# The smaller expert's second product moved ahead of the larger expert's last first products, with its load, in a two-block transformer kernel

## The reference

```
logits = t @ router                        # t: 256 x 1024, 8 experts
top_vals, top_idx = top_k(logits, 2)
gates = softmax(top_vals) placed at top_idx
for e in range(8):
    h_e = silu(t @ w1[e]) * (t @ w3[e])    # 1024 -> 3584
    out = out + gates[:, e] * (h_e @ w2[e])  # 3584 -> 1024
```

## Time and profile before

| what | value |
|---|---|
| median of three timed runs | 2823.32 us |
| profiled execution, its own time | 2816.06 us |
| span of that execution (first to last instruction) | 2814.2 us |
| PE busy (products) | 2723.3 us, 97% |
| DVE busy | 1684.4 us, 60% |
| ACT busy | 462.1 us, 16% |
| mean DMA rate over the span | 220 GB/s |
| chain that ended last, by engine | PE 86%, DVE 7%, DMA 4% |

### The profile page before, as it was taken

How to read it: one execution, slowest core, us unless ns; L and a number is a source line. 1 busy time by engine, 2 the same in 40 slices (tenths; PEclk the granted TensorE clock), 3 DMA queues, 4 the chain that set the end, 5 groups by cost and what they waited for, 6 DMA issues and landing times.

```text
span 2814.2 us, 48541 instructions
## 1 busy us (share of the span) xinstructions
PE 2723.3 (97%) x20880; PEld 2086.3 (74%) x20880; DVE 1684.4 (60%) x2934; ACT 462.1 (16%) x914; POOL 91.0 (3%) x130
## 2 busy tenths in 40 slices
PE   7999999999999999999998999988999999999997
PEld 6689878776678978777776887557777777777775
DVE  2554155776365416587554674237778878878876
ACT  2230212101212111200133111211111111111111
POOL 0011300000001120000000000000000000000000
PEclk9999999999999999999999999989999999999999
DMA  6242342543333135344333343329999999999995
GB/s 240 97 150 75 127 159 104 203 179 151 113 118 117 72 128 187 141 174 160 123 146 133 150 180 114 130 96 390 418 385 384 416 389 383 416 395 377 413 415 233
DMA packets 56940, 617.88 MB, mean 220 GB/s; under 512 B 6544, under 2 KB 6800, under 8 KB 8720
## 3 DMA queue, kind: packets, MB, share of 16 engines
q1 hardware_dynamic: 54576, 603.27, 54.5%
q0 software_dynamic: 2144, 11.45, 1.0%
HBM read 613.64 MB, written 1.05 MB: 218 GB/s over the span
## 4 chain that ended last, share of the span: by engine, by line
PE 86%; DVE 7%; DMA 4%; ACT 1%; issue 1%; SPq 0%; DVEq 0%; ACTq 0%
PE ps L1552 11%; PE ps L750 11%; PE ps L1232 10%; PE ps L1101 8%; PE ps L1244 8%; PE ps L1562 7%; PE ps L1576 5%; PE ps L1081 4%; PE ps L773 3%; PE ps L1598 3%; PE ps L731 2%; PE ps L1113 2%; DMA fbT<-in_od_exp_w 2%; PE ps L816 1%; PE ps L1210 1%; PE ps L1252 1%
## 5 line engine op out<-in xcount | busy, mean ns | idle before, releaser
L1101 PE MATMUL ps<-hT,slabA 128*128 128x256 f32 x1024 | 232.0, 380 | 1.1 <-ACT work L1837 1.1
L1101 PEld LDWEIGHTS ps<-hT,slabA 128*128 128x128 f32 x1024 | 192.2, 190 | 28.3 <-ACT work L1837 1.9
L1562 PE MATMUL ps<-fbT,work 128*64 128x256 f32 x1792 | 205.7, 382 | 2.8 <-DMA fbT<-in_od_exp_w 2.8
L1562 PEld LDWEIGHTS ps<-fbT,work 128*64 128x64 f32 x1792 | 124.1, 137 | 70.3 <-issue 11.0
L1552 PE MATMUL ps<-prm,hT 128*64 128x128 f32 x2688 | 167.4, 273 | 3.6 <-DVE resets L2965 2.9
L750 PE MATMUL ps<-hT,slabA 128*128 128x256 f32 x736 | 165.7, 385 | 1.0 <-DMA slabA<-in_od_w_in 0.5
L1552 PEld LDWEIGHTS ps<-prm,hT 128*64 128x64 f32 x2688 | 150.7, 136 | 13.6 <-issue 4.0
L750 PEld LDWEIGHTS ps<-hT,slabA 128*128 128x128 f32 x736 | 140.6, 193 | 21.6 <-issue 1.4
L1232 PEld LDWEIGHTS ps<-work 128*128 128x128 f32 x1152 | 139.5, 192 | 21.5 <-issue 21.0
L1232 PE MATMUL ps<-work 128*128 128x128 f32 x1152 | 143.9, 275 | 0.1
L750 PE MATMUL ps<-slabA,hT 128*128 128x512 f32 (+2 forms) x416 | 141.5, 496 | 2.2 <-ACT work L2024 1.8
(11 more groups left out here) (448 smaller groups left out, 4564.7 us busy)
## 6 DMA issues: line engine op xcount, KB each, us to landing
slabA<-in_od_exp_w SPq DMA_DIRECT2D x56, 2048.0 KB, 11.7
fbT<-in_od_exp_w SPq DMA_DIRECT2D x56, 2048.0 KB, 9.8
slabB<-in_od_exp_w SPq DMA_DIRECT2D x56, 1024.0 KB, 11.2
fbT<-in_od_exp_w SPq DMA_DIRECT2D x56, 1024.0 KB, 11.9
slabA<-in_w_in SPq DMA_DIRECT2D x24, 2048.0 KB, 8.2
slabA<-in_mlp_w SPq DMA_DIRECT2D x16, 2048.0 KB, 9.6
slabB<-in_mlp_w SPq DMA_DIRECT2D x32, 1024.0 KB, 4.8
slabA<-in_ev_ffn_w SPq DMA_DIRECT2D x11, 2048.0 KB, 7.9
```

Source lines behind the costliest of these rows:

```text
L1101: last = mm(ps[:, b, 0:T], side["gates"][:, k, c % 4 * P:(c % 4 + 1) * P], hT[:, k, :], start=(k == 0), stop=(k == KD - 1))
L1562: last = mm(ps[SMALL * j:SMALL * (j + 1), 1, 0:2 * P].rearrange("p (w n) -> p w n", w=2), xs[:, k, :], v[:, k, :, j * P:(j + 1) * P], star ...
```

## The change

The diff has three parts. On PE `down_b(g - 1)` moves from the end of a step to the place behind `up_b(g)`; its wait for `hidden_b` stands in it in every step, and the one in `extra` goes. In SP's queue `down_slab(g, 1)`, the load of B's second weights, moves from the last place of a step to the one behind the load of B's first weights. And in the first step `up_b(0)` no longer comes first: it runs inside `up_a(0, 0)`, behind the two products without sums and ahead of the wait for `sums_ready`.

```
@@ SyncE's queue
             for g in range(PAIRS * UPS):
                 up_slab(g + 1, 1)
+                down_slab(g, 1)
                 up_slab(g + 2, 0)
                 down_slab(g + 1, 0)
-                down_slab(g, 1)
@@ up_a
                     if c == 2 and part == 0:
+                        if g == 0:
+                            up_b(g)
                         pe.wait_ge(sem("sums_ready"), due("pe", "sums_ready"))
@@ down_b
-                if (g + 1) % UPS not in extras(g + 1):
-                    pe.wait_ge(sem("hidden_b"), due("pe", "hidden_b"))
+                pe.wait_ge(sem("hidden_b"), due("pe", "hidden_b"))
@@ extra
-                if i in extras(g):
-                    pe.wait_ge(sem("hidden_b"), due("pe", "hidden_b"))
@@ the steps on PE
                     if g == 0:
                         pe.wait_ge(sem("slots_a"), due("pe", "slots_a"))
-                        up_b(g)
                     up_a(g, 0)
                     if g:
                         turn(g - 1)
...
                     if g:
                         up_b(g)
+                        down_b(g - 1)
                     extra(g)
                     up_a(g, 1)
                     if g:
                         down_a(g - 1)
-                        down_b(g - 1)
```

## The result

Four runs of the changed kernel gave 2850.57 to 2854.46 us, median 2852.36; before, in four runs, 2823.33. The ratio is 1.0099 with a 95% interval of 1.0081 to 1.0116, so the change costs 29 us (23 to 33). The forecast was 2844, with a range of 2833 to 2856. Two runs of experiment 1, at 3270.75 and 4072.37 us with a mean granted clock of 0.82 and 0.65, are in none of the comparisons. The two profiled executions lie further apart, 2851.62 against 2816.06 us; of that distance of 35.6 us, 2.7 are there before the first expert is loaded (its first load is issued at 1892.67 us before and at 1895.36 after), in code that the change leaves alone.

What follows compares the result with a forecast made beforehand. PE was taken to set the step, with the loop through DVE and the transfers close behind; 22.1 + 3.9 + 0.9 + 1.0 - 3.7 - 2.8 = +21.4 us on the median 2823.3 gave 2844.7, stated as 2844, range 2833 to 2856.

Steps and rivals of the forecast that it cites:

- (d): Join on DVE: A's slab, issued D (sums' end) + 10.68, leaves 0.8 us spare; three pick steps add +1.0 us.
- (e): PE's nine short waits of B's second products for weights, and one for sums, go: -3.7 us (bounds -0.9, -4.2).
- (f): Tail: B's last second weights load earlier, DVE sets the order: -2.8 us, or -1.3 if the clock falls.
- (a): Steps 2 to 55: loop through ACT and DVE overruns its spare time by 0.41 us a step, +22.1 us.
- (b): Three scatter steps, where PE waits for DVE's y: each grows by the whole 1.72 us; +3.9 us beyond (a).
- (c): Start of B's second products: wait for hidden_b 0.3 us late only behind sums_of_slots, in 3 steps, +0.9 us.
- (g): First step: c = 0, 1 can start earlier, but sums still set c = 2; 0 us (bounds -0.3, +0.5).
- The third rival: A's slab, behind 1 MB more in the queue, sets the step: 16.2 us each, 2889 us; chance 0.05.
- the first (transfers pace the steps, 2813 us): Transfers set the step in the timed runs, and B's earlier load removes waits: 2813 us; chance 0.05.
- The second (the move does not reach the join): DVE comes late to the join for other reasons, so (a) is 0: 2821 us; chance 0.05.
- the fourth, the clock: A pause in each step drops PE to the half rate: 2908 us and more; chance 0.01.

Runs made afterwards that it cites:

- experiment 1: Changed kernel, c = 2 waiting only for the first two sums, sums of slots first in the first step: median 2827.8 us, ratio to before 1.001.
- experiment 6: Changed kernel with the old first step, B's first products first again: 2854.68 us, ratio to before 1.0104.
- experiment 5: Kernel before, B's second products moved from the step's end into the next step, behind c = 1: 2822.86 us, ratio 0.9999.
- Experiment 2: Changed kernel, loading only the first half of B's second weights in each step: 2844.47 us, ratio to before 1.0077.
- experiment 7: Kernel before, B's very last second weights loaded into the buffer of B's first weights: 2820.76 us, ratio 0.9984.
- the third kernel: Changed kernel with the load of B's second weights back in its old last place in SP's queue: 3060.51 us, ratio 1.0844.

## Why the prediction was right

The sign, the place and the plain step were right; one term was far off in size, (d), and two a little, (e) and (f). Time between the loads of c = 2 in step 1 and in step 55 was 851.0 us before and is 884.8 after, in the profiles. The sum by its own parts:

| part | forecast | in the profiles |
|---|---|---|
| (a) loop, steps 2 to 55 | +22.1 | +21.7 (53 steps of 0.40, one of 0.46) |
| (b) scatter steps | +3.9 | +3.9 (22.43 for 20.72) |
| (c) wait for hidden_b | +0.9 | +0.7 (3 of 0.24) |
| (d) late joins | +1.0 | +9.7 (11 steps) |
| (e) waits that go | -3.7 | -2.2 (what is left) |
| c = 2 of step 1 to c = 2 of step 55 | +24.2 | +33.8 |
| (f) tail | -2.8 | -1.0 |
| (g) first step | 0 | 0 (experiment 6) |

**(a)** holds by the timeline, by experiment 1, which took the loop away and with it the 0.40, and by experiment 5, which left the loop its cover. **(b)** The scatter's first products now wait longer for DVE's y:

```profile
2155.05 3.27 PE L1636 MATMUL ps<-work 64*128 64x512 f32 x14 [1.68 <-DVE work L3007]
```

1.68 us where it was 0.36: 1.32 more. **(c)** In the steps behind `sums_of_slots` the loads of B's second products stand right behind the copy:

```profile
2341.55 0.29 DVE L2979 COPY work<-ps 128x128 f32<-128x128 f32 x1
2341.96 0.23 PEld L1599 LDWEIGHTS ps<-fbT,work 128*64 128x64 f32 x4 [0.46 <-issue]
```

**(d)** is the term that was mis-sized, by 8.7 us. The term as I put it was: A's slab issued at D + 10.68, today's 12.27 us to landing although 1 MB more is ahead of it, DVE at the join 0.8 us before it has to be, and only three steps with picks late, by 0.66. The issue came as forecast, at D + 10.63. Step g = 3 of the changed kernel shows what was wrong:

```profile
1965.32 1.23 DVE L2957 TENSOR_TENSOR prm<-slabA 128x1024 f32<-128x1024 f32 x1 [3.98 <-DMA slabA<-in_od_exp_w]
...
1968.16 0.67 DVE L2892 TENSOR_SCALAR work<-cst,fbT 128x64 f32<-128x64 f32 x2
1968.86 0.73 DVE L2915 TENSOR_SCALAR work<-cst,fbT 128x128 f32<-128x128 f32 x2
1969.62 0.43 DVE L2992 TENSOR_TENSOR work<-work 128x256 f32<-128x256 f32 x1
```

The slab comes 9.17 us after the sums (1956.15), not 7.60, and the join runs 13.47 after them, where 11.15 is ACT's pace: 2.3 us lost in one step. In the four steps i = 3 (the fourth has gates but no picks) it was 2.3, 0.9, 2.2 and 1.5, in seven others 0.1 to 0.9. In these eleven steps the slab took 12.4 to 13.9 us to land, 13.2 on the mean, not 12.27. Estimated from these rows, with 12.27 in each the joins would be late by 3.1 us in all; the other 6.6 of the 9.7 are the slower landing, which I had put at nothing. Experiment 2, with half a megabyte less ahead of the slab, brings it down to 0.75, so the transfers cause the late joins. The third rival priced this delay, at 2.4 us a step, and it came in part: 0.5 us on the median of all steps, 1.0 on the mean of these eleven. And the joins were late before too, by 11.4 us in all, of which 1.3 us of spare time took all but 0.3: the change spent the spare time, so a delay of the slab, old or new, now counts in full.

**(e)** In the profile before, five steps are longer for waits for weights, by 1.8 us in all, and late sums add 0.3. So the nine short waits, taken at 3.5 us, were worth about half of it; the lower bound given was 0.9. **(f)** was right as a mechanism and off by the clock: -1.0, a little outside its second bound of -1.3. (That bound set 3.29 us of the timeline against 1.72 of the chain; in one view, the timeline, the 8 products take 1.94 us at the full clock, so a fallen clock costs 1.35 there, not 1.57.) The tail of the changed kernel, and its granted clock in a window (0.76):

```profile
2820.81 0.49 ACT L2081 ACTIVATE work<-ps 128x384 f32<-128x384 f32 x1 [4.06 <-PE ps L1554]
...
2827.06 0.29 DVE L2979 COPY work<-ps 128x128 f32<-128x128 f32 x1
...
2827.50 2.57 PE L1599 MATMUL ps<-fbT,work 128*64 128x512 f32 x8 [2.78 <-DVE work L2979]
...
2829.78 2.64 PE L1578 MATMUL ps<-slabB,work 128*64 128x256 f32 x12
```

```profile
2826.00:2833.00 7.00, 5.50 (x28) 3.29 (x30) 3.29 (x9) 0.00 (x0) 0.00 (x0) 0.76 0.00 0
```

A's last products begin 8.97 us after ACT's start (8.30 forecast, 12.78 before), and run for a time at 1.2 GHz.

**(g)** In the first step the products without sums did start early and gained nothing; PE only waits longer at c = 2, 1.46 us where it was 0.68:

```profile
1908.19 1.97 PE L1554 MATMUL ps<-slabA,work 128*64 128x128 f32 x32 [2.04 <-DVE work L2934]
...
1915.07 1.97 PE L1554 MATMUL ps<-prm,hT 128*64 128x128 f32 x32 [1.46 <-DVE resets L2963]
```

In the timed runs the change costs 29 us, where the profiles give 35.6, or 32.9 without the 2.7 us from ahead of the experts, which are chance. The profiled execution of before is its fastest, with 2816.06 us where 29 timed runs lie between 2818.24 and 2831.26. The profile of experiment 7, whose kernel is that of before up to its last load, has 855.0 us from step 1 to step 55 where before has 851.0, 1.6 of the difference in step 1, where the clock fell. That slower runs of before wait longer for weights, which the changed kernel wouldn't, is likely but not shown. So there is luck in the number: the sum was +21.4, with bounds of 16 to 32, and the profiles have +32.9, just outside; the timed runs, with 29, lie nearer to it for a reason that stays open.

Of the rivals, the first (transfers pace the steps, 2813 us) fell with the sign and with experiments 1 and 2: the transfers cost 8 to 10 us here, and do not set the plain step. The second (the move does not reach the join) fell with the plain step, where the join still follows ACT's start by 0.59 us. The third came in part, under (d), and the fourth, the clock, did not come in the steps. One sign was weak: DVE's wait ahead of the join, forecast above 1.5 us, is 1.79 in the plain step shown, but by the waits lists only 1.51 on the mean of 43, where it was 1.36 of 42 before; the slab came too late for more.

## What to carry to other kernels

Before work is moved inside a loop that one engine fills, look for the shortest chain that leaves that engine and comes back to it, and count what the engine does meanwhile: work moved out of that stretch is paid for as soon as the spare time is used up, in every round, though the engine's total is the same. And spare time has other users: list the delays that it hides now, for they come due with it. And a load with more bytes put ahead of it does not keep its time to landing: that is a term of its own. A wait for the last of several results, where the first would do, is the cheapest thing to look for in such a chain.

## What the runs showed of the hardware that was not expected

The clock of TensorE held through at least 0.41 us of waiting in each of 54 steps (1.00 granted over the stage). Longer waits came before both outcomes. In the changed kernel it held through waits of the products of 2.24 us in step 1, 2.50 in step 4 and 2.39 in step 32 (all at 1.00), and in experiment 7 through 1.57 us ahead of the last products. It fell in the tail of the changed kernel, in which PE waited 2.78 us (the 8 products took 2.57 us for 1.94), and in experiment 1 with 2.08 us of waiting in a scatter step. Even the same wait went both ways: ahead of step 1's sums PE waits 2.23 us in the kernel before and 2.24 in experiment 7, and the stretch behind the wait was granted 1.00 in the one and 0.72 in the other (windows, first before, then experiment 7):

```profile
1922.00:1928.00 6.00, 5.30 (x63) 4.03 (x65) 5.59 (x13) 0.60 (x1) 0.00 (x0) 1.00 0.99 418
1927.00:1933.00 6.00, 5.96 (x55) 4.59 (x57) 4.97 (x12) 0.60 (x1) 0.00 (x0) 0.72 0.98 414
```

In the third kernel, 14 of 51 waits of 1.9 to 4.4 us left the products at 1.94 us and 37 did not, and the mean clock over the execution was 0.968. So a wait of 2 us and more can cost a second time, in the work behind it, and its length alone does not tell whether it will. The Trainium skill, "TensorE: Matmul & The Clock Gate", Part 1, has the half rate as the state that idling brings back; the runs agree for these waits, and the rival built on it for 0.41 us a step did not come.
